# Running a heavy and a light expert of a mixture-of-experts kernel together, block by block in turns

## The chip, the cores and the metric

The kernel runs on one core of a Trainium2 chip. The metric is device time in microseconds (us) from start to end of one execution; lower is better. Engines are named as in the profile: PE is TensorE's matmul stream, DVE is VectorE, ACT is ScalarE, POOL is GpSimd and SP is SyncE, which here issues the loads of the weights.

## The reference

Two layers of an encoder over 256 tokens of width 1024. Each layer is a token mixer and then a channel mixer; the second layer's channel mixer sends each token to 2 of 8 experts. The change touches only those experts:

```python
def swiglu(h, w1, w3, w2):
    return (jax.nn.silu(h @ w1) * (h @ w3)) @ w2
...
    for e in range(N_EXPERTS):
        out = out + combine[..., e:e + 1] * swiglu(h, w1[e], w3[e], w2[e])
```

An expert has w1 and w3 of 1024 x 3584 and w2 of 3584 x 1024, all in float32.

## The kernel before

The experts are ordered by load and run as eight phases with the roles `ROLES = "HLHLHLHH"`: a heavy phase (H: 0, 2, 4, 6, 7) has 128 slots for tokens, a light one (L: 1, 3, 5) has 64. The hidden width of 3584 is cut into `NM` = 7 blocks of 512. A block needs w1 (two halves), w3 (two halves) and w2 (two halves): six **items** of 128 x 2048 floats, 1 MiB each, so 336 items in all.

Each item goes through four steps. SP loads it into one of 7 buffers `raw`. ACT copies it, rounded, to `whi`, line L1726. DVE computes the remainder `wlo` = raw - whi, line L2381. PE then multiplies with both. `whi` and `wlo` have only `SPLIT` = 3 buffers each, so ACT may write `whi` of item n only when PE has finished item n - 3, and SP may reload a `raw` buffer when the `wlo` of item n - 7 is done.

The number of matmuls of an item depends on the role. In a heavy phase the tokens' rows are split into a high and a low part, and an item takes 12 matmuls of 128 x 512 (hi x whi, lo x whi, hi x wlo). In a light phase both parts of the 64 rows lie side by side in the 128 columns, and an item takes 8 (L1187, L1191 for w1 and w3, L1230 for w2).

PE goes through the blocks in the order: w1 of block b (bank 0, group "e1"), transpose of the hidden values of block b - 1 (bank 2, "eT"), w3 of block b (bank 1, "e3"), w2 of block b - 1 (`down`, banks 4 and 5). Between them the other two engines work:

- heavy: ACT applies silu to bank 0 (L1737), DVE multiplies with bank 1 (`hidden`, L2394, the row `sgv<-sgv,bank`), PE transposes (L1210), ACT makes the high part (L1752), DVE the low part (`hidden_lo`, L2417, the row `yT_lo<-bank,yT_hi`). `down` waits for that low part before its first matmul, and for `wlo` of its own item.
- light: ACT copies bank 0 and bank 1 to SBUF (L1737, L1747), PE transposes and folds the 64-row halves together with 16 small matmuls (L1206), ACT applies silu (L1742), and DVE makes both parts with three instructions (L2407, L2410, L2412), which `down` waits for.

Which item each engine handles before which of these steps is set by `e_room`: an engine takes all items whose `whi` can become free before PE reaches the step in question. All engines work strictly through the order written in the program. In particular `hidden_lo` first does the `wlo` of every item up to three after the last one that PE finishes ahead of the transpose.

Between two experts, the new tokens' rows come back from memory (a DMA on ACT's queue), are transposed by PE (`rows_T`, L1250) and split by ACT and DVE; the old expert's result is copied out of banks 4 and 5 by ACT (L1845), for a light one folded by PE (`fold_result`, L1242) and copied again, and stored by a DMA on ACT's queue.

Of the kernel before, what the change touches and what calls it, by code (L numbers as in the profile page):

```python
# [42 lines left out]
CAP = 128  # L43
# [9 lines left out]
TWO_PI = 6.283185307179586  # L53

# [8 lines left out]
def plan_psum(depth, heads, x_heads, fcd, nblk, over_jobs):  # L63
# [16 lines left out]
    for l in range(depth):  # L80
# [69 lines left out]
        else:  # L150
# [14 lines left out]
            for p in range(last + 1):  # L165
                for b in range(1, nblk):
                    give(p, "e1", b, 0)
                    if b == 1 and p and ROLES[p - 1] == "L":
                        for n in range(2):
                            give(p - 1, "yf", n, 6 + n)  # L170
                    give(p, "eT", b - 1, 2)
                    if b == nblk - 1 and p < last:
                        for n in range(2):
                            give(p + 1, "rows", n, 7 - n)
                    give(p, "e3", b, 1)
                    if b == 1:
                        for n in range(2):
                            give(p, "ey", n, 4 + n)
                if p < last:
                    give(p + 1, "e1", 0, 0)  # L180
                    give(p, "eT", nblk - 1, 2)
                    give(p + 1, "e3", 0, 1)
                else:
                    give(p, "eT", nblk - 1, 2)
                    give(p, "selT", 0, 3)
                    for n in range(4):
                        give(p, "scatter", n, n)
# [59 lines left out]
def build(nc, x, mem, positions, g_mix, w_in, g_q, g_kv, w_uq, w_uk, w_uv, g_sg, w_s, b_s, g_mem,  # L247
# [31 lines left out]
    with ExitStack() as ctx:  # L279
# [105 lines left out]
        hselT = [v[:, :, 2:4, :].rearrange("p n a s -> p n (a s)") for v in yT]  # L385

# [92 lines left out]
        slots_moved = sem("slots_moved")  # L479
# [94 lines left out]

        e_items = head_items(0)
        for p in range(NE):
            e_items += mid_items(p) + (head_items(p + 1) if p < LAST else []) + halves(p, ("w2", NM - 1))
# [99 lines left out]
        def e_room(phase, kind, n):  # L677

            limit = marks[phase, kind, n][0]
            start, end = (N_E, N_E + PER_E) if phase == "over" else (0, N_E)  # L680
            i = start + SPLIT
            while i < end and marks["item", i - SPLIT][0] < limit:
                i += 1
            return i

# [12 lines left out]
        def _(pe):  # L698
# [470 lines left out]
            def up(phase, kind, b_, j=0, rows=None):  # L1169
# [3 lines left out]
                for half in range(2):  # L1173
# [10 lines left out]
                    for k, a in order:  # L1184
                        if rows is not None and phase == 0 and k == 0:
                            rows(half) if a else pe.wait_ge(rows_hi, half + 1)
                        nc.tensor.matmul(b[:, :], hselT[a][:, half, tok(k)], w[:, k, :],  # L1187
                                         start=(half + k + a == 0), stop=False)
                    w = e_part(wlo, lo_ready, n, j)
                    for k in range(4):  # L1190
                        ins = nc.tensor.matmul(b[:, :], hselT[0][:, half, tok(k)], w[:, k, :],  # L1191
# [21 lines left out]
            def down(phase, b_, j=0, halves=(0, 1)):  # L1213
# [6 lines left out]
                for half in halves:  # L1220
# [24 lines left out]
            def rows_T(phase, j=0):  # L1245

                for n in range(2):
                    b = claim((phase, "rows", n), j)
                    for c in range(4):
                        ins = nc.tensor.transpose(b[:, c * CAP:(c + 1) * CAP], row_in_slot[:, tok(4 * n + c)], ident[:, :])  # L1250
                    mark(ins, (phase, "rows", n))

            def blocks(phase, j=0):

                for b_ in range(1, NM):
                    up(phase, "w1", b_, j)
                    if b_ == 1 and phase != "over" and phase and light[phase - 1]:
                        fold_result(phase - 1)
                    hidden_T(phase, b_ - 1, j)
                    if phase != "over" and phase < LAST and b_ == NM - 1:  # L1260

                        pe.wait_ge(slots_moved, 32 * phase + 16)
                        rows_T(phase + 1)
# [47 lines left out]
            with pe.If(overflow > 0):  # L1311
                before, names = count, set(marks)
                with pe.Fori(0, OVER) as j:
                    pe.wait_ge(slots_moved, 16 * j + 16 * (2 * NE - 1))
                    rows_T("over", j)
# [83 lines left out]
        def _(pool):  # L1399
# [69 lines left out]
            pool.wait_ge(slots_moved, 32 * (NE - 1))  # L1469
# [7 lines left out]
        def _(act):  # L1477
# [276 lines left out]
            def rows_hi_part(phase, j=0):  # L1754

                for n in range(2):
                    b = full(act, (phase, "rows", n), j)
                    if is_light(phase):
                        ins = nc.scalar.activation(by_slot(hselT[0][:, n, :])[:, :, 0:LIGHT],
                                                   by_slot(b[:, :])[:, :, 0:LIGHT], ACT.Copy)  # L1760
                    else:
                        ins = nc.scalar.activation(hselT[0][:, n, :], b[:, :], ACT.Copy)
                    ins.then_inc(rows_hi, 1)

            def store_result(p):

                if light[p]:
# [3 lines left out]
                    for n in range(2):  # L1771
                        read(act, (p, "yf", n))
                else:
                    for n in range(2):
                        read(act, (p, "ey", n))
                act.dma_start(y_by_slot[p], y_slot).then_inc(slots_moved, 16)

            def blocks(phase, j=0):

                for b_ in range(1, NM):  # L1780
                    e_hi(e_room(phase, "e1", b_), j)
                    if is_light(phase):
                        e_hi(e_room(phase, "eT", b_ - 1), j)
                        silu_folded(phase, b_ - 1)
                    e_silu(phase, b_, j)
                    if b_ == 1 and phase != "over" and phase and light[phase - 1]:
                        store_result(phase - 1)
                    if phase != "over" and phase < LAST and b_ == (4 if phase else 5):

                        act.wait_ge(dispatched, 16 * 2 * T)  # L1790
                        if phase:
                            reached(act, (phase, "rows", 1))
                        act.dma_start(row_in_slot, rows_by_slot[phase + 1]).then_inc(slots_moved, 16)
                    e_hi(e_room(phase, "eT", b_ - 1), j)
                    if is_light(phase):
                        e_hi(e_room(phase, "e3", b_))
                        copy_gate(phase, b_)
                    else:
                        hidden_hi(phase, b_ - 1, j)
# [23 lines left out]
            for p in range(NE - 1):  # L1823
                blocks(p)

                e_hi(e_room(p, "e3", NM - 1))
                reached(act, (p, "e3", NM - 1))
                rows_hi_part(p + 1)
                e_hi(e_room(p + 1, "e1", 0))
                if light[p]:  # L1830
                    e_hi(e_room(p, "eT", NM - 1))
                    silu_folded(p, NM - 1)
                e_silu(p + 1, 0)
                if not light[p]:
                    e_hi(e_room(p, "eT", NM - 1))
                    hidden_hi(p, NM - 1)
                if light[p + 1]:
                    e_hi(e_room(p + 1, "e3", 0))
# [751 lines left out]
```

## Time and profile before

| | us |
|---|---|
| median of 3 runs | 1623.9 (1622.59 to 1624.29) |
| the profiled execution | 1622.44 |
| its span | 1620.6 |
| PE / DVE / ACT busy | 1576.3 / 1278.0 / 1057.4 |
| experts 1 to 6, from w1 of expert 1 to the first half of w3 of expert 7 | 678.55 |

The profiled execution's own time is 1.84 us above its span and 1.5 us below the median. Matmul busy times overlap in the profile: what counts for PE is the distance from the start of one instruction to the start of the next. The last line of the table is the part of the program that the change reorders.

### The profile page before, as it was taken

The numbers are of one execution on the slowest core, as the hardware profiler recorded it, in microseconds if no ns is written. First come the engines' busy times: TensorE is split into PE (matmuls) and PEld (weight loads), VectorE is DVE, ScalarE is ACT, GpSimd is POOL, SyncE is SP. The second block draws the span as 40 slices with busy tenths as digits, with TensorE's granted clock in tenths as the row PEclk, the third lists the DMA queues.
The fourth block names the chain that finished last, engine by engine and source line by source line (L and its number), as shares of the span: only waits on it lengthen the run. The fifth ranks groups of instructions, "written<-read, shape, count | busy, mean of one in ns | idle before, by whom it ended". The sixth has DMA issues, their size and how long they took to land.

```text
span 1620.6 us, 21022 instructions
## 1 busy us (share of the span) xinstructions
PE 1576.3 (97%) x8224; PEld 1335.5 (82%) x8224; DVE 1278.0 (79%) x1204; ACT 1057.4 (65%) x988; POOL 28.6 (2%) x69
## 2 busy tenths in 40 slices
PE   9999999999999999999999999989999999999997
PEld 8988888999989888787877788777788777788885
DVE  7575666555576756689899988899888999888997
ACT  6555445333355554567788877788777888777774
POOL 1000000000000000001000000000000000000100
PEclk9999999999999999999999999999999999999998
DMA  7754478977455535669999999999999999999992
GB/s 239 223 185 142 143 250 279 303 245 233 127 165 174 181 117 182 250 259 364 423 421 420 421 419 391 368 422 420 422 398 374 401 420 421 412 394 352 409 397 114
DMA packets 143112, 497.48 MB, mean 307 GB/s; under 512 B 8534, under 2 KB 64400, under 8 KB 100000
## 3 DMA queue, kind: packets, MB, share of 16 engines
q1 hardware_dynamic: 137008, 479.23, 78.1%
q0 software_dynamic: 2624, 8.45, 1.5%
q10 hardware_dynamic: 3376, 8.39, 1.4%
q8 instruction: 68, 1.11, 0.3%
q14 instruction: 36, 0.29, 0.0%
HBM read 476.64 MB, written 19.40 MB: 306 GB/s over the span
## 4 chain that ended last, share of the span: by engine, by line
PE 71%; DVE 20%; ACT 4%; issue 4%; DMA 1%; ACTq 0%; POOL 0%; DVEq 0%; POOLq 0%
PE bank L730 21%; DVE wlo L2381 14%; PE bank L1187 14%; PE bank L1230 13%; PE bank L901 9%; PE bank L1191 7%; ACT whi L1726 2%; ACT whi L1493 1%; PE bank L720 1%; DVE wlo L1915 1%; PE bank L1015 1%; PE bank L1210 1%; PE bank L1206 1%; DMA hn<-in_mem 1%; ACT pbuf L1628 0%
## 5 line engine op out<-in xcount | busy, mean ns | idle before, releaser
L2381 DVE TENSOR_TENSOR wlo<-raw,whi 128x2048 fp32r<-128x2048 f32 x328 | 738.9, 2286 | 67.4 <-ACT whi L1726 67.1
L1726 ACT ACTIVATE whi<-raw 128x2048 fp32r<-128x2048 f32 x328 | 624.0, 1917 | 161.5 <-PE bank L1191 83.8
L1915 DVE TENSOR_TENSOR wlo<-raw,whi 128x2048 fp32r<-128x2048 f32 (+3 forms) x121 | 259.3, 2148 | 178.6 <-ACT whi L1493 177.2
L1187 PE MATMUL bank<-whi,yT_hi 128*128 128x512 f32 x896 | 311.9, 396 | 0.0
L1493 ACT ACTIVATE whi<-raw 128x2048 fp32r<-128x2048 f32 (+3 forms) x121 | 217.8, 1801 | 137.7 <-PE bank L730 101.3
L1191 PE MATMUL bank<-wlo,yT_hi 128*128 128x512 f32 x896 | 240.5, 390 | 0.1
L1187 PE MATMUL bank<-whi,yT_lo 128*128 128x512 f32 x560 | 216.5, 390 | 0.0
L1230 PE MATMUL bank<-whi,yT_hi 128*128 128x512 f32 x448 | 180.4, 403 | 26.1 <-DVE yT_hi L2412 16.0
L1191 PEld LDWEIGHTS bank<-wlo,yT_hi 128*128 128x128 f32 x896 | 167.8, 188 | 36.9 <-DVE wlo L2381 1.4
L1187 PEld LDWEIGHTS bank<-whi,yT_hi 128*128 128x128 f32 x896 | 166.7, 188 | 33.1
L1230 PE MATMUL bank<-wlo,yT_hi 128*128 128x512 f32 x448 | 175.9, 393 | 0.0
L1230 PEld LDWEIGHTS bank<-whi,yT_hi 128*128 128x128 f32 x448 | 84.6, 189 | 61.7 <-DVE yT_hi L2412 23.8
L730 PE MATMUL bank<-hT_hi,whi 128*128 128x256 f32 x464 | 131.4, 283 | 0.0
L730 PE MATMUL bank<-hT_hi,wlo 128*128 128x256 f32 x464 | 131.3, 283 | 0.0
L730 PE MATMUL bank<-hT_lo,whi 128*128 128x256 f32 x464 | 131.3, 283 | 0.0
L1187 PEld LDWEIGHTS bank<-whi,yT_lo 128*128 128x128 f32 x560 | 105.2, 188 | 21.2 <-DVE yT_lo L2298 0.2
L1230 PE MATMUL bank<-whi,yT_lo 128*128 128x512 f32 x280 | 109.1, 390 | 0.0
L1230 PEld LDWEIGHTS bank<-wlo,yT_hi 128*128 128x128 f32 x448 | 84.7, 189 | 16.9
L730 PEld LDWEIGHTS bank<-hT_lo,whi 128*128 128x128 f32 x464 | 89.0, 192 | 0.4
L730 PEld LDWEIGHTS bank<-hT_hi,whi 128*128 128x128 f32 x464 | 89.0, 192 | 0.4
L730 PEld LDWEIGHTS bank<-hT_hi,wlo 128*128 128x128 f32 x464 | 89.0, 192 | 0.0
L730 PE MATMUL bank<-whi,mT_hi 128*128 128x512 f32 (+1 forms) x204 | 79.6, 390 | 0.0
(323 smaller groups left out, 2059.2 us busy)
## 6 DMA issues: line engine op xcount, KB each, us to landing
raw<-in_moe_w SPq DMA_DIRECT2D x336, 1024.0 KB, 8.5
raw<-in_w_in SPq DMA_DIRECT2D x36, 1024.0 KB, 5.2
raw<-in_dense_w SPq DMA_DIRECT2D x30, 1024.0 KB, 6.6
raw<-in_w_br SPq DMA_DIRECT2D x12, 1024.0 KB, 5.0
rows_by_slot<-qxT SPq DMA_DIRECT2D x23, 512.0 KB, 7.2
raw<-in_w_out SPq DMA_DIRECT2D x8, 1024.0 KB, 5.0
raw<-in_w_mkv SPq DMA_DIRECT2D x6, 1024.0 KB, 8.4
cqkv<-rows_by_slot ACTq DMA_DIRECT2D x7, 512.0 KB, 7.9
```

The lines of the kernel that those rows point to most:

```text
L720: ins = nc.tensor.matmul(bank, lhs(k), rhs(k), start=(k == 0), stop=(k == n - 1))
L730: ins = nc.tensor.matmul(bank, lhs(a, k), rhs(b, k), start=(start and k == chunks[0] and a + b == 0), stop=(stop and k == chunks[-1] and a ...
L901: ins = nc.tensor.matmul(bank, src(a, x0), w[b_][:, w0, :], start=(start and q + i == 0), stop=(stop and last))
L1015: ins = nc.tensor.matmul(b[:, t * SEQ:(t + 1) * SEQ], qT[0:QK, h, tok(t)], kT[0:QK, h, :], start=True, stop=True)
L1187: nc.tensor.matmul(b[:, :], hselT[a][:, half, tok(k)], w[:, k, :], start=(half + k + a == 0), stop=False)
L1191: ins = nc.tensor.matmul(b[:, :], hselT[0][:, half, tok(k)], w[:, k, :], start=False, stop=(half == 1 and k == 3))
L1206: ins = nc.tensor.matmul(b[:, a:a + LIGHT], src[:, tok(c)], fold[:, 0:LIGHT], start=True, stop=True)
L1230: ins = nc.tensor.matmul(banks[4 + n][:, :], gated_m[a][:, b_ % 2, tok(2 * half + c)], w[p][:, c, n * HALF:(n + 1) * HALF], start=(b_ + ha ...
L1493: nc.scalar.activation(whi[:, m % SPLIT, 0:floats(n)], raw[:, pieces[n][1], 0:floats(n)], ACT.Copy).then_inc(hi_ready, 1)
L1726: nc.scalar.activation(whi[:, (E0 + n) % SPLIT, :], raw[:, n % RAW, :], ACT.Copy).then_inc(hi_ready, 1)
L1915: V.tensor_tensor(wlo[:, m % SPLIT, 0:size], raw[:, pieces[n][1], 0:size], whi[:, m % SPLIT, 0:size].bitcast(F32), ALU.subtract).then_inc( ...
L2381: V.tensor_tensor(wlo[:, s, :], raw[:, n % RAW, :], whi[:, s, :].bitcast(F32), ALU.subtract).then_inc(lo_ready, 1)
```

## The change

Phase 0 runs alone as before. Then phases 2 and 1 run together: block 0 of 2, block 0 of 1, block 1 of 2, block 1 of 1 and so on; then 4 and 3, then 6 and 5; phase 7 stands alone. Within a step PE's pattern stays: w1 of the new block, transpose of the block before it in the new order, w3 of the new block, w2 of the block before. Since both phases of a pair are live, the light one has its own buffers for its rows (`lselT`, `light_row`) and accumulates its result in banks 6 and 7 instead of 4 and 5, and the rows' transposes use bank 3. The semaphore for rows and results is split into three. The number of items, matmuls and bytes stays as it was. In phase 7 the four `add_picked` of DVE stand one block later.

```diff
+def block_order(nblk):
+    order = [(0, b) for b in range(nblk)]
+    for p in range(1, len(ROLES) - 1, 2):
+        order += [(q, b) for b in range(nblk) for q in (p + 1, p)]
+    return order + [(len(ROLES) - 1, b) for b in range(nblk)]
+
+def row_steps(nblk):
+    order = block_order(nblk)
+    mid, late = {}, {}
+    for p in range(1, len(ROLES)):
+        s = order.index((p, 0))
+        if s == nblk:
+            mid.setdefault(s - 1, []).extend([(p, 0), (p, 1)])
+        else:
+            late.setdefault(s - 2, []).append((p, 0))
+            mid.setdefault(s - 1, []).append((p, 1))
+    return mid, late
...
+        lselT = mT[0][:, 0:4, :].rearrange("p (n a) s -> p n (a s)", n=2)
+        light_row = qxT[:, :, :].rearrange("p k s -> p (k s)")
...
-        for p in range(NE):
-            e_items += mid_items(p) + (head_items(p + 1) if p < LAST else []) + halves(p, ("w2", NM - 1))
+        for (p, b), (q, c) in zip(order, order[1:]):
+            e_items += halves(q, ("w1", c), ("w3", c)) + halves(p, ("w2", b))
+        e_items += halves(LAST, ("w2", NM - 1))
...
-                                ins = nc.tensor.matmul(banks[4 + n][:, :], gated_m[a][:, b_ % 2, tok(2 * half + c)],
+                                ins = nc.tensor.matmul(banks[(6 if is_light(phase) else 4) + n][:, :], gated_m[a][:, b_ % 2, tok(2 * half + c)],
...
-            for p in range(NE):
-                blocks(p)
-                if p < LAST:
-                    up(p + 1, "w1", 0, 0, lambda half: read(pe, (p + 1, "rows", half)))
-                    hidden_T(p, NM - 1)
-                    up(p + 1, "w3", 0)
-                    down(p, NM - 1)
+            for i in range(1, SINGLE + 1):
+                (p, b_), (q, c) = order[i - 1:i + 1]
+                up(q, "w1", c, 0, None if c else lambda half: read(pe, (q, "rows", half)))
+                if folded(i) is not None:
+                    fold_result(folded(i))
+                hidden_T(p, b_)
+                for r, n in mid_rows.get(i, []):
+                    rows_T(r, n)
+                up(q, "w3", c)
+                for r, n in late_rows.get(i, []):
+                    rows_T(r, n)
+                down(p, b_)
+            blocks(LAST)
...
+            for i in range(1, SINGLE + 1):
+                (p, b_), (q, c) = order[i - 1:i + 1]
+                e_lo(e_room(q, "e1", c))
...
+                hidden_lo(p, b_)
...
+                e_lo(e_room(q, "e3", c))
...
+                hidden(q, c)
```

What this does to DVE's order, first **before, inside a heavy expert** (`sgv` is the product `hidden`, `yT_lo` the low part that `down` waits for; one block is a product, five `wlo`, a low part, one `wlo`):

```order
L2381 TENSOR_TENSOR wlo<-raw,whi 128x2048 x5
L2417 TENSOR_TENSOR yT_lo<-bank2,yT_hi 128x512
L2381 TENSOR_TENSOR wlo<-raw,whi 128x2048
L2394 TENSOR_TENSOR sgv<-sgv,bank1 128x512
L2381 TENSOR_TENSOR wlo<-raw,whi 128x2048 x5
```

Here the six `wlo` of a block are all of heavy items. DVE **before, inside a light expert** (one block is the three instructions of the light hidden values and six `wlo`):

```order
L2407 TENSOR_TENSOR cT<-cT,bank2 128x256
L2410 CAST yT_hi<-cT 128x4x64
L2412 TENSOR_TENSOR yT_hi<-cT,yT_hi 128x4x64
L2381 TENSOR_TENSOR wlo<-raw,whi 128x2048 x6
L2407 TENSOR_TENSOR cT<-cT,bank2 128x256
```

**After, inside a pair** (one turn of a heavy and a light block):

```order
L2458 TENSOR_TENSOR sgv<-sgv,bank1 128x512
L2445 TENSOR_TENSOR wlo<-raw,whi 128x2048 x5
L2481 TENSOR_TENSOR yT_lo<-bank2,yT_hi 128x512
L2445 TENSOR_TENSOR wlo<-raw,whi 128x2048 x6
L2471 TENSOR_TENSOR cT<-cT,bank2 128x256
L2474 CAST yT_hi<-cT 128x4x64
L2476 TENSOR_TENSOR yT_hi<-cT,yT_hi 128x4x64
L2445 TENSOR_TENSOR wlo<-raw,whi 128x2048
L2458 TENSOR_TENSOR sgv<-sgv,bank1 128x512
```

The first `wlo` run behind `sgv` here is of items w1 and w3 of the light block and the first half of w2 of the heavy one; then comes the heavy block's low part. So between the product and the low part of a heavy block five `wlo` stand as before, but four of them now belong to a light block, whose matmuls are fewer. The single `wlo` ahead of `sgv` is the second half of w2 of the light block, as it was of the heavy block before. The six in between are the second half of w2 of the heavy block, w1 and w3 of the next heavy block, and the first half of w2 of the light block.

ACT's order **before, inside a light expert** (`cT` is the folded silu, `sgv<-bank0` and `sgv<-bank1` the copies of e1 and e3):

```order
L1742 ACTIVATE cT<-bank2 128x256
L1737 ACTIVATE sgv<-bank0 128x512
L1726 ACTIVATE whi<-raw 128x2048
L1747 ACTIVATE sgv<-bank1 128x512
L1726 ACTIVATE whi<-raw 128x2048 x5
```

and **after, inside a pair** (`sgv<-bank0` is the heavy block's silu, then the light block's copy; `yT_hi` the heavy block's high part):

```order
L1793 ACTIVATE cT<-bank2 128x256
L1788 ACTIVATE sgv<-bank0 128x512
L1777 ACTIVATE whi<-raw 128x2048 x5
L1788 ACTIVATE sgv<-bank0 128x512
L1777 ACTIVATE whi<-raw 128x2048
L1803 ACTIVATE yT_hi<-bank2 128x512
L1777 ACTIVATE whi<-raw 128x2048
L1798 ACTIVATE sgv<-bank1 128x512
L1777 ACTIVATE whi<-raw 128x2048 x5
```

The run of five `whi` is one turn's second half of w2 of the light block and the next light block's w1 and w3; the single ones are the two halves of w2 of the heavy block. The small instructions of both roles now stand in one queue in turns.

## Rows read from the trace of the kernel before

**Rows 1.** The page: span; busy time, its share of the span and instructions of PE

```profile
span 1620.6 us, 21022 instructions
...
PE 1576.3 (97%) x8224; PEld 1335.5 (82%) x8224; DVE 1278.0 (79%) x1204; ACT 1057.4 (65%) x988; POOL 28.6 (2%) x69
```

**Rows 2.** Busy time by stretch: experts 1 to 6, inside heavy 2, inside light 3

```profile
core 0: us, PE busy (x) PEld busy (x) DVE busy (x) ACT busy (x) POOL busy (x), PEclk, DMA share, GB/s
811.46:1489.90 678.44, 653.00 (x3041) 530.76 (x3040) 622.99 (x373) 542.77 (x392) 0.00 (x0) 1.00 1.00 405
944.00:1028.00 84.00, 84.00 (x384) 69.64 (x385) 73.66 (x40) 61.86 (x40) 0.00 (x0) 1.00 1.00 400
1060.00:1118.00 58.00, 53.16 (x257) 42.56 (x257) 57.69 (x39) 49.36 (x37) 0.00 (x0) 1.00 1.01 422
```

**Rows 3.** Chain that ended last (start, length, work): two heavy, then two light blocks

```profile
994.63 5.44 PE bank L1230 x24
...
1011.44 5.44 PE bank L1230 x24
...
1060.63 10.40 DVE wlo L2381 x5
...
1074.96 10.36 DVE wlo L2381 x5
```

**Rows 4.** Timeline (start, length, work, wait): heavy expert, next item starts, whi, wlo

```profile
1189.23 0.39 PE L1187 MATMUL bank<-whi,yT_hi 128*128 128x512 f32 x1
...
1189.49 1.92 ACT L1726 ACTIVATE whi<-raw 128x2048 fp32r<-128x2048 f32 x1 [0.80 <-PE bank L1230]
...
1191.44 2.29 DVE L2381 TENSOR_TENSOR wlo<-raw,whi 128x2048 fp32r<-128x2048 f32 x1 [0.42 <-ACT whi L1726]
```

**Rows 5.** Timeline, step from light expert 1 to heavy expert 2

```profile
919.37 1.89 PE L1206 MATMUL bank<-cT,sgv 128*128 128x64 f32 x16
...
921.07 0.48 PE L1187 MATMUL bank<-whi,yT_hi 128*128 128x512 f32 x1
...
926.13 2.29 DVE L2381 TENSOR_TENSOR wlo<-raw,whi 128x2048 fp32r<-128x2048 f32 x1 [0.95 <-ACT whi L1726]
...
928.34 0.68 DVE L2394 TENSOR_TENSOR sgv<-sgv,bank 128x512 f32<-128x512 f32 x1
...
928.94 4.49 DVE L2381 TENSOR_TENSOR wlo<-raw,whi 128x2048 fp32r<-128x2048 f32 x2
```

**Rows 6.** Timeline, step from heavy expert 2 to light expert 3

```profile
1022.60 1.04 PE L1250 MATMUL bank<-ident,cqkv 128*128 128x128 f32 x8
...
1023.39 0.48 PE L1187 MATMUL bank<-whi,yT_hi 128*128 128x512 f32 x1
...
1034.39 1.07 PE L1187 MATMUL bank<-whi,yT_hi 128*128 128x512 f32 x4
...
1034.65 3.73 ACT L1726 ACTIVATE whi<-raw 128x2048 fp32r<-128x2048 f32 x2 [0.80 <-PE bank L1230]
...
1036.60 6.70 DVE L2381 TENSOR_TENSOR wlo<-raw,whi 128x2048 fp32r<-128x2048 f32 x3 [0.21 <-ACT whi L1726]
...
1043.22 0.68 DVE L2417 TENSOR_TENSOR yT_lo<-bank,yT_hi 128x512 fp32r<-128x512 f32 x1
...
1043.96 0.50 PE L1230 MATMUL bank<-whi,yT_hi 128*128 128x512 f32 x1 [1.60 <-DVE yT_lo L2417]
```

**Rows 7.** Timeline, fold and store of light expert 1's result

```profile
935.94 1.88 PE L1242 MATMUL bank<-mv,cT 128*128 128x512 f32 x4
...
938.97 1.92 ACT L1726 ACTIVATE whi<-raw 128x2048 fp32r<-128x2048 f32 x1 [0.52 <-ACT mv L1770]
```

**Rows 8.** Groups by line, 790 to 1600 us: result copies

```profile
L1845 ACT ACTIVATE mv<-bank 128x512 f32<-128x512 f32 x14 | 7.9, 586 | 1.0 <-PE bank L1230 1.0
```

**Rows 9.** Timeline: w1 of expert 1; first half of expert 7's w3 ends

```profile
811.46 1.07 PE L1187 MATMUL bank<-whi,yT_hi 128*128 128x512 f32 x4
...
1490.01 0.39 PE L1187 MATMUL bank<-whi,yT_hi 128*128 128x512 f32 x1
```

More of the change, by code:

```diff
@@ L164, in plan_psum @@
             give(0, "e3", 0, 1)
[L165 to L187, printed above, removed]
+            order = block_order(nblk)
+            mid, late = row_steps(nblk)
+            for i in range(1, len(order)):
+                (p, b), (q, c) = order[i - 1:i + 1]
+                give(q, "e1", c, 0)
+                if i > 1 and order[i - 2][1] == nblk - 1 and ROLES[order[i - 2][0]] == "L":
+                    for n in range(2):
+                        give(order[i - 2][0], "yf", n, 6 + n)
+                give(p, "eT", b, 2)
+                for r, n in mid.get(i, []):
+                    give(r, "rows", n, 7 - n if i == nblk - 1 else 3)
+                give(q, "e3", c, 1)
+                for r, n in late.get(i, []):
+                    give(r, "rows", n, 3)
+                if b == 0:
+                    for n in range(2):
+                        give(p, "ey", n, (6 if ROLES[p] == "L" else 4) + n)
+            give(last, "eT", nblk - 1, 2)
+            give(last, "selT", 0, 3)
+            for n in range(4):
+                give(last, "scatter", n, n)
             start = list(used)
@@ L684, in e_room, with rows_at, fetched, folded @@
             return i
+        def rows_at(p):
+            return (lselT if light[p] else hselT[0]), sum(light[q] == light[p] for q in range(1, p + 1))
+        def fetched(p):
+            return order.index((p, 0)) - 4 if p > 2 else NM - 2
+        def folded(i):
+            p, b = order[i - 2] if i > 1 else (0, 0)
+            return p if b == NM - 1 and light[p] else None
+        nth_rows, n_rows = {}, T
+        for i in range(len(order)):
+            for name in mid_rows.get(i, []) + late_rows.get(i, []):
+                n_rows += 1
+                nth_rows[name] = n_rows
         def light_block(p, b):
@@ L1243, in fold_result, with rows_T @@
                          (p, "yf", n))
[L1245 to L1251, printed above, removed]
+            def rows_T(phase, n, j=0):
+                if phase != "over":
+                    pe.wait_ge(light_row_in if light[phase] else heavy_row_in, 16 * rows_at(phase)[1])
+                row = light_row if is_light(phase) else row_in_slot
+                b = claim((phase, "rows", n), j)
+                for c in range(4):
+                    ins = nc.tensor.transpose(b[:, c * CAP:(c + 1) * CAP], row[:, tok(4 * n + c)], ident[:, :])
+                mark(ins, (phase, "rows", n))
             def blocks(phase, j=0):
@@ L1752, in hidden_hi, with rows_hi_part @@
                 nc.scalar.activation(gated_m[0][:, b_ % 2, :], b[:, :], ACT.Copy).then_inc(g_hi, 1)
[L1754 to L1763, printed above, removed]
+            def rows_hi_part(phase, n, j=0):
+                b = full(act, (phase, "rows", n), j)
+                if is_light(phase):
+                    ins = nc.scalar.activation(by_slot(lselT[:, n, :])[:, :, 0:LIGHT], by_slot(b[:, :])[:, :, 0:LIGHT], ACT.Copy)
+                else:
+                    ins = nc.scalar.activation(hselT[0][:, n, :], b[:, :], ACT.Copy)
+                ins.then_inc(rows_hi, 1)
+            n_stored = 0
             def store_result(p):
+                nonlocal n_stored
+                kind = "yf" if light[p] else "ey"
                 if light[p]:
@@ L1781, in blocks @@
                     e_hi(e_room(phase, "e1", b_), j)
-                    if is_light(phase):
-                        e_hi(e_room(phase, "eT", b_ - 1), j)
-                        silu_folded(phase, b_ - 1)
                     e_silu(phase, b_, j)
[L1786 to L1793, printed above, removed]
-                    e_hi(e_room(phase, "eT", b_ - 1), j)
[L1795 to L1799, printed above, removed]
+                    if phase == LAST and b_ == 1:
+                        store_result(folded(SINGLE + 1))
+                    e_hi(e_room(phase, "eT", b_ - 1), j)
+                    hidden_hi(phase, b_ - 1, j)
                     if phase == LAST and b_ == 3:
@@ L2401, in hidden_lo @@
                 b = full(dve, (phase, "eT", b_), j)
-                count = NM * (NE if phase == "over" else phase) + b_ + 1 + NM * j
+                count = NM * NE + b_ + 1 + NM * j if phase == "over" else order.index((phase, b_)) + 1
                 if is_light(phase):
@@ L2533, in _ @@
                     select()
-                    rows_lo("over", j)
+                    for n in range(2):
+                        rows_lo("over", n, j)
                     n_done = N_E
```

186 lines of the change are left out of this document (109 added, 77 removed).

## The prediction

> **What bounds the kernel now.** I read the page first: PE is busy for 97% of the span [rows 1], which says little, because the busy times of pipelined matmuls overlap. The stretches come next. Inside heavy expert 2 PE is busy for all of 84 us and DVE for 74; inside light expert 3 DVE is busy for 57.69 of 58 us and PE for 53 [rows 2]. So the two kinds of expert have different limits, and the chain of waits says the same with the length of a block: heavy blocks hang on PE and repeat every 1011.44 - 994.63 = 16.81 us, light ones hang on DVE and repeat every 1074.96 - 1060.63 = 14.33 us [rows 3]. A heavy and a light block cost 31.14 us. The moves between experts come on top: experts 1 to 6 take 1490.01 - 811.46 = 678.55 us [rows 9], and 21 x 31.14 is 654 of them.
>
> The pieces of a block. A matmul of the experts takes 5.44 / 24 = 0.227 us from start to start [rows 3], so a heavy item (12) takes 2.72 us of PE and a light one (8) 1.81. The heavy transpose takes the rest, 16.81 - 6 x 2.72 = 0.49 us. The light transpose takes 921.07 - 919.37 = 1.70, and the matmul behind it starts up some 0.09 late, as the one at 1043.96 does (0.50 long instead of 0.39) [rows 5, 6]: 1.79. An item's way to PE: the next item starts at 1189.23, `whi` starts 0.26 later, takes 1.92, and `wlo` starts 0.03 behind it [rows 4]: 2.21 us from the end of item n - 3 to the start of `wlo` of n. Back to back, `wlo` follow each other every (6.70 - 2.29) / 2 = 2.205 us [rows 6], a small instruction starts 2.21 behind the start of a `wlo`, and `sgv` holds the next `wlo` up by 928.94 - 928.34 = 0.60 [rows 5].
>
> **What the change does to a turn.** It removes and adds no item, matmul or byte; all it does is order. I number a turn's items as PE takes them: 1 to 4 are w1 and w3 of the light block, 5 and 6 w2 of the heavy one, 7 to 10 w1 and w3 of the next heavy block, 11 and 12 w2 of the light one. The heavy transpose lies between 2 and 3, the light one between 8 and 9.
>
> Added up per engine a turn looks cheap. PE: 6 x 1.81 + 6 x 2.72 + 0.49 + 1.79 = 29.5 us. DVE: 12 x 2.205 = 26.5, two heavy steps of 0.60, and 14.33 - 6 x 2.205 = 1.10 for the light step, 28.8 us. DMA: 12.58 MB at the 422 GB/s that it moves in the light expert [rows 2] is 29.8 us. All are below 31.14.
>
> But three buffers hold the engines close together, and there is a loop of waits that a turn can't be shorter than. By the order after the change:
>
> 1. `whi` of 12 must wait until PE has finished 9; its `wlo` starts 2.21 us after that.
> 2. Behind it DVE has, in this order, the heavy product (2.21 after the start of `wlo` 12), `wlo` of 1 to 5 (0.60 for the product, four times 2.205, then 2.21), and the heavy low part (0.68 [rows 6]): 2.21 + 0.60 + 8.82 + 2.21 + 0.68 = 14.52 us without a gap.
> 3. PE's item 5 waits for that low part (0.06 to the start at 1043.96 [rows 6], 0.10 start-up). Then PE does 5, 6, 7, 8, the light transpose and 9: 0.16 + 5 x 2.72 + 1.79 = 15.55 us. And 9 releases the next turn's `whi` 12.
>
> The loop is 2.21 + 14.52 + 15.55 = **32.3 us a turn, against 31.14 now**: 1.14 us more. It mixes the slow leg of each kind: DVE at its full pace for seven instructions, then PE at the heavy pace while DVE waits for `whi`. Inside heavy blocks it can't arise, since there the six items past the product take PE 16.3 us and DVE is always early; inside light ones DVE never stops, so nothing but its own sum counts.
>
> Is step 2 really without a gap, and is nothing else later? With PE's end of 9 at 0: `whi` of 1 is ready at 4.9 (10 ends at 2.72), DVE wants it at 5.0. 11 ends at 4.5, 12 waits for its `wlo` and ends at about 6.4, so `whi` of 2, 3 and 4 are ready at 6.8, 8.7 and 10.7; DVE wants them at 7.2, 9.4 and 11.6. ACT then copies the light e1, which ends at 10.5 (about as long as a result copy, 0.59 [rows 8]), and has `whi` of 5 at 13.3; wanted at 13.8. PE ends item 4 at 14.9 and stands still until 16.8: 1.9 us in each turn. After that the `wlo` of 6, 7 and 8 are done 0.7 us or more before PE needs them. The light step's three instructions end about 2 us before PE wants 11. Loads: a turn of 32.3 us takes 390 GB/s, less than the 422 that the light expert draws, so no wait on DMA is added.
>
> This wait exists once already, at the step from a heavy to a light expert: `whi` at 1034.65, three `wlo` from 1036.60, low part at 1043.22, and PE stands for 1.60 us until 1043.96 [rows 6]. The order there is that of every turn from now on. It is the nearest row to the new case, and it is 1.60 rather than 1.9 because the two items before it were heavy ones.
>
> **The sum.** Up to the w1 at 811.46 little differs: four more row transposes for the second expert, half of 1023.39 - 1022.60 [rows 6], 0.4 us. From there to the end of 9 in expert 2: 2 x 2.72 + 0.49 + 2.72, and four row transposes: 9.1. Then 21 turns: 21 x 32.27 = 677.7. Surcharges at the ends of experts:
> - first turn: items 11 and 12 are heavy (the low part is then due 9.5 us after the end of 12 at 8.16, so 0.9 late), and two result copies of 0.59 [rows 8] delay `whi` of 3: 2.1.
> - each of the two changes of pair: row transposes, their high and low parts, and bank 3 that has to come free in between, on all three legs (I follow the order: +1.0 on DVE, because ACT's row copy holds up `whi` of 1; +1.15 at item 5; +0.4 behind 8): 2.6. In the next turn result copies and the fold, where `whi` comes 938.97 - 935.94 = 3.03 us after the fold's start [rows 7], so that of 5 is 1.6 late. 4.2 each, 8.4.
> - into expert 7: 1.0.
>
> Together 0.4 + 9.1 + 677.7 + 2.1 + 8.4 + 1.0 = 698.7 against 678.55: +20.2. Behind it the last `down` of the pair is a light one (-1.8), and the fold of expert 5 comes into expert 7 (1.72 from 935.94, and about 0.3): +0.2. With the profiled execution's own time, 1622.44 + 20.4 = 1642.8; from the median it is **1644 us**, 1.3% slower.
>
> Bounds. The surcharges have no row of their own: if they cost nothing the time is 11.5 us less, about 1632; if they cost twice what I say, 11.5 more, 1656. The loop itself is bounded from below by its own instructions, all of which have rows; what it may have on top is a few hand-overs of 0.03 to 0.3 us like those of an item's way to PE [rows 4].
>
> **A rule that says the opposite.** The rows show two regimes, one on PE and one on DVE [rows 2, 3]. The Trainium skill, page "Perfetto Trace Analysis", section "Optimization Strategy", says of kernels whose most-contended engine changes over time that performance may be improved by interleaving those regimes. That is this change, and it is the first rival. The sum by the rule would be that of the busiest resource; by the loop above it is not reached with three buffers.
>
> **Rivals.**
> 1. *The loads even out.* A turn costs its busiest sum, DMA's 29.8 us. For it: the three sums, all below 31.14. Then 21 x 29.8 = 625.8 + 21.0 is 646.8, 32 us less: 1592. It would need `whi` to run further ahead than item n - 3, and the row of 1.60 us [rows 6] speaks against it. The change pays as soon as a turn with its surcharges stays under 31.3 us. 4%.
> 2. *The single steps repeat as they are recorded.* The step to a light expert takes 15.1 us (1034.39 until item 6 ends at 1043.96 + 5.54), the one to a heavy expert, by its pieces, 4 x 2.72 + 1.79 + 2 x 1.81 + 0.1 = 16.4; a turn would be 31.5, if DVE came into each turn as early as it does there. That gives 21 x 0.8 less than my sum: 1628. Against it: items 11 and 12 are light in a turn, so PE reaches 5 sooner than DVE. 5%.
> 3. *More than the loop.* If the pauses of PE lowered its granted clock, or ACT, which alternates between both roles, came later than I follow, the turn would go to 33 us or more: 1660 and up. The granted clock is 1.00, the 2.4 GHz level, in the light expert too, where PE has 5 of 58 us free [rows 2]. 5%.
>
> **How the numbers follow.** The forecast has 86%; its range 1632 to 1657 comes from the surcharges, and I give 1631 to 1658, which leaves out about 2 in 10. A measurement tells 0.2% (3 us) from no change. Faster 0.05 (rival 1 and a little of rival 2), within 0.2% 0.04, slower 0.91.
>
> **What would show it.** In the chain of the changed kernel, landmarks in the middle of a pair should repeat every 32.3 us. PE should show a pause before the first matmul of the heavy `down` in each turn, put down to `yT_lo`, of 1.6 to 2 us, some 21 times, where it can occur only at the three steps from heavy to light now; `wlo` of 1 to 5 should stand back to back, and DVE should wait for `whi` in items 8 to 12. DVE should no longer be busy for all of any long stretch, and DMA's rate should lie at about 390 GB/s in the pairs. I am wrong if turns repeat under 31.2 us, if the pause stands elsewhere, or if the difference arises outside the pairs.

## The result, and the profile after

The changed kernel takes **1650.39 us** (median of 4 runs, 1648.31 to 1655.48), the kernel before 1623.36 (4 runs, 1622.59 to 1624.29): 1.0171 times as long, 95% interval 1.0158 to 1.0184. The forecast was 1644, with a range of 1631 to 1658. The profiled execution is the shortest of the four, 1648.31, and stands 25.9 us above that of before.

The page: span and busy times.

```profile
span 1646.5 us, 21021 instructions
...
PE 1588.0 (96%) x8224; PEld 1332.7 (81%) x8224; DVE 1279.9 (78%) x1204; ACT 1056.7 (64%) x988; POOL 29.1 (2%) x69
```

Against [rows 1] the page hardly moves: the same matmuls and the same work on DVE, and busy times within 12 us on PE and 2 on DVE, in a span that is 25.9 us longer. The stretches say more. Inside the pair of experts 2 and 1, and inside that of 4 and 3:

```profile
core 0: us, PE busy (x) PEld busy (x) DVE busy (x) ACT busy (x) POOL busy (x), PEclk, DMA share, GB/s
835.00:1000.00 165.00, 156.04 (x712) 123.76 (x712) 148.90 (x88) 127.65 (x89) 0.00 (x0) 1.00 0.98 393
1070.00:1235.00 165.00, 155.75 (x704) 123.64 (x705) 147.32 (x88) 126.34 (x88) 0.00 (x0) 0.99 0.98 390
```

Nothing is busy all the time any more: PE for 94 to 95%, DVE for 89 to 90%. DMA moves 390 to 393 GB/s. In [rows 2] PE was full in the heavy expert and DVE in the light one. The two regimes are mixed, and neither engine gained by it. The chain of waits (start, length, work), at the first matmuls of the heavy `down` in seven turns:

```profile
840.47 5.74 PE bank L1276 x24
872.81 5.74 PE bank L1276 x24
905.14 5.73 PE bank L1276 x24
937.47 5.74 PE bank L1276 x24
...
1070.84 7.34 PE bank L1276 x24
1104.77 5.74 PE bank L1276 x24
1137.11 5.73 PE bank L1276 x24
```

A turn takes 872.81 - 840.47 = 32.34 us, then 32.33, 32.33; where [rows 3] give 16.81 + 14.33 = 31.14 for the same two blocks. The row of 7.34 us is an exception, told below. One turn of the same chain, from item 9's last matmuls to item 5, shows which leg holds which:

```profile
1119.59 0.93 PE bank L1237 x4
1120.61 1.93 ACT whi L1777
1122.59 2.17 issue
1124.76 0.68 DVE sgv L2458
1125.44 8.64 DVE wlo L2445 x4
1134.09 0.08 issue
1134.17 2.29 DVE wlo L2445
1136.45 0.61 DVE yT_lo L2481
```

And the timeline of the same stretch, with what ended each wait:

```profile
1120.61 1.92 ACT L1777 ACTIVATE whi<-raw 128x2048 fp32r<-128x2048 f32 x1 [1.88 <-PE bank L1237]
...
1122.55 2.29 DVE L2445 TENSOR_TENSOR wlo<-raw,whi 128x2048 fp32r<-128x2048 f32 x1 [1.15 <-ACT whi L1777]
...
1124.76 0.68 DVE L2458 TENSOR_TENSOR sgv<-sgv,bank 128x512 f32<-128x512 f32 x1
...
1125.36 11.09 DVE L2445 TENSOR_TENSOR wlo<-raw,whi 128x2048 fp32r<-128x2048 f32 x5
...
1136.37 0.68 DVE L2481 TENSOR_TENSOR yT_lo<-bank,yT_hi 128x512 fp32r<-128x512 f32 x1
...
1137.11 0.50 PE L1276 MATMUL bank<-whi,yT_hi 128*128 128x512 f32 x1 [1.60 <-DVE yT_lo L2481]
```

ACT waits 1.88 us for PE's item 9 before the `whi` of 12, DVE 1.15 us for that `whi`; then DVE's `wlo` of 12, the product, the `wlo` of 1 to 5 and the low part follow without a gap, and PE has stood still for 1.60 us when the low part comes. PE's next five items and the light transpose, 1104.77 to 1120.52, release the next `whi`. The waits over 840 to 1500 us (engine, line, waited for: us in total, times, longest) put numbers on all turns together:

```profile
ACT whi L1777 <- PE bank L1237: 81.7, 75, 2.3
DVE wlo L2445 <- ACT whi L1777: 70.3, 100, 2.3
...
PE bank L1276 <- DVE yT_lo L2481: 31.0, 19, 2.0
```

PE's pause before the heavy `down` occurs 19 times and costs 31.0 us, 1.63 each. At the two changes of pair it lies ahead of the rows' transposes, which stand before `down` there (2.16 us each).

### The profile page after: what moved, and what is told of

It reads as the page before. It is cut to its first block, busy times and chain, and to the rows that moved or that the text cites. A ratio compares the mean times of both kernels' runs of the same rounds, so it can differ in the third digit from the quotient of the medians.

```text
span 1646.5 us, 21021 instructions
## 1 busy us (share of the span) xinstructions
PE 1588.0 (96%) x8224; PEld 1332.7 (81%) x8224; DVE 1279.9 (78%) x1204; ACT 1056.7 (64%) x988; POOL 29.1 (2%) x69
## 3 DMA queue, kind: packets, MB, share of 16 engines
q0 software_dynamic: 2624, 8.45, 1.5%
## 4 chain that ended last, share of the span: by engine, by line
PE 69%; DVE 20%; issue 5%; ACT 5%; ACTq 0%; DVEq 0%; POOL 0%; POOLq 0%
PE bank L776 22%; DVE wlo L2445 14%; PE bank L1233 12%; PE bank L1276 12%; PE bank L947 9%; PE bank L1237 6%; ACT whi L1777 3%; PE bank L1252 2%; ACT whi L1544 1%; DVE yT_lo L2481 1%; PE bank L766 1%; DVE wlo L1979 1%; PE bank L1061 1%; DVE sgv L2458 1%; ACT pbuf L1679 0%
## 5 line engine op out<-in xcount | busy, mean ns | idle before, releaser
L1233 PE MATMUL bank<-whi,yT_hi 128*128 128x512 f32 x560 | 219.8, 396 | 0.0
L1276 PE MATMUL bank<-whi,yT_hi 128*128 128x512 f32 x448 | 180.9, 404 | 32.3 <-DVE yT_lo L2481 31.9
L1276 PE MATMUL bank<-wlo,yT_hi 128*128 128x512 f32 x448 | 176.2, 393 | 0.0
L1237 PE MATMUL bank<-wlo,yT_hi 128*128 128x512 f32 x560 | 150.3, 390 | 0.0
L1276 PEld LDWEIGHTS bank<-whi,yT_hi 128*128 128x128 f32 x448 | 84.9, 189 | 65.6 <-DVE yT_lo L2481 42.4
L1237 PEld LDWEIGHTS bank<-wlo,yT_hi 128*128 128x128 f32 x560 | 105.0, 188 | 22.8 <-DVE wlo L2445 0.5
L1233 PEld LDWEIGHTS bank<-whi,yT_hi 128*128 128x128 f32 x560 | 105.2, 188 | 20.9
L1276 PEld LDWEIGHTS bank<-wlo,yT_hi 128*128 128x128 f32 x448 | 85.1, 190 | 17.6
L1237 PE MATMUL bank<-wlo,mT_hi 128*128 128x512 f32 x336 | 95.7, 406 | 2.9 <-DVE wlo L2445 1.2
L1233 PE MATMUL bank<-whi,mT_hi 128*128 128x512 f32 x336 | 92.4, 397 | 0.0
```

The source lines that it names most:

```text
L1233: nc.tensor.matmul(b[:, :], (lselT if is_light(phase) else hselT[a])[:, half, tok(k)], w[:, k, :], start=(half + k + a == 0), stop=False)
L1237: ins = nc.tensor.matmul(b[:, :], (lselT if is_light(phase) else hselT[0])[:, half, tok(k)], w[:, k, :], start=False, stop=(half == 1 and ...
L1276: ins = nc.tensor.matmul(banks[(6 if is_light(phase) else 4) + n][:, :], gated_m[a][:, b_ % 2, tok(2 * half + c)], w[p][:, c, n * HALF:(n ...
```

## The experiments

**1 to 3: a fourth `whi` buffer.** The loop of waits exists because `whi` of 12 may not be written before 9 is done. With four buffers it may be written once 8 is done. The fourth lies in a tile that is unused in this stage (`mT_lo`); `wlo` keeps three, so DVE now waits itself for item n - 3. The same edit in the kernel before is the control.

```diff
+        def hi_user(n):
+            return n - (4 if HEAD + EARLY + 3 <= n < N_E else SPLIT)
...
-                        reached(act, ("item", n - SPLIT), j)
-                    nc.scalar.activation(whi[:, (E0 + n) % SPLIT, :], raw[:, n % RAW, :], ACT.Copy).then_inc(hi_ready, 1)
+                        reached(act, ("item", hi_user(n)), j)
+                    nc.scalar.activation(whi_of(n), raw[:, n % RAW, :], ACT.Copy).then_inc(hi_ready, 1)
...
+                    if n < N_E:
+                        reached(dve, ("item", n - SPLIT))
```

The second of the three also moves ACT's copy of the light e1 behind the `whi` of item 5:

```diff
-                e_silu(q, c)
+                if not light[q]:
+                    e_silu(q, c)
...
+                if light[q]:
+                    e_silu(q, c)
```

Expected of the changed kernel with four `whi`:

> The changed kernel with a fourth buffer for whi (a tile that the experts don't use); wlo keeps three, so DVE now waits for PE's end of item n - 3 itself. The order of the instructions is as in the changed kernel. Loop of waits: whi of 12 is made while PE is still at 9, so wlo of 12 starts about 0.3 instead of 2.2 us behind the end of 9. Then ACT's copy of the light e1, which stands ahead of whi of 5 and waits for PE's item 2, is the next to hold: turn about 31.2 us instead of 32.3, time about 1626, with a shorter pause ahead of the heavy w2. Loads even out (rival): the buffers were never the limit and the turn stays at 32.3, about 1650. If the surplus was the granted clock alone: also about 1650.

Expected with the copy moved too:

> As the one before, and ACT's copy of the light e1 stands behind whi of item 5. Loop of waits: DVE's leg runs from 0.35 us behind the end of 9 without a gap, turn 30.4 us, about 40 us less than the changed kernel, 1609, which is faster than the kernel before. If the loads' sum of 29.8 us on DMA holds earlier, a turn of 30.5 or more and DVE waiting for ACT that waits for DMA. Rival (loads or clock): no change, 1650.

Expected of the control:

> Control: the kernel before with the same fourth buffer for whi. Heavy blocks hang on PE (16.81) and light ones on DVE (14.33), and neither waits for a buffer, so both stay. Only the three pauses at the steps from heavy to light go, 1.6 to 1.8 us each: about 1618. If a fourth buffer is worth as much here as in the pairs (rival: it helps everywhere), 1590 to 1600.

Measured, against 1623.13 of before: 1626.54 with four `whi` (1624.95 to 1629.98; ratio 1.0023, 1.0013 to 1.0032), 1620.97 with the copy moved (1619.40 to 1622.31; 0.9985, 0.9976 to 0.9995), and 1618.93 for the control (1617.82 to 1620.28; 0.9972, 0.9961 to 0.9983). So one more buffer takes 24 us off the changed kernel and 4 off the one before. That is the cause, taken away: the change's loss was the loop through `whi`. The timeline of DVE with four `whi`, low parts in two turns:

```profile
1096.01 0.68 DVE L2493 TENSOR_TENSOR yT_lo<-bank,yT_hi 128x512 fp32r<-128x512 f32 x1
...
1127.14 0.68 DVE L2493 TENSOR_TENSOR yT_lo<-bank,yT_hi 128x512 fp32r<-128x512 f32 x1
```

A turn takes 31.13 us, 1.20 less than 32.33, and 21 turns make 25.2 us. Its two changes of pair give 3.3 of them back: they cost 7.4 us each over two plain turns, where the changed kernel's cost 11.5 together. That leaves 21.9, where the two profiled executions lie 21.8 apart. What holds the turn now is in the rows between them, on ACT and DVE, ahead of the low part of 1127.14:

```profile
1122.49 0.60 ACT L1798 ACTIVATE sgv<-bank 128x512 f32<-128x512 f32 x1 [1.65 <-PE bank L1247]
1122.98 1.91 ACT L1787 ACTIVATE whi<-raw 128x2048 fp32r<-128x2048 f32 x1
...
1124.93 2.29 DVE L2457 TENSOR_TENSOR wlo<-raw,whi 128x2048 fp32r<-128x2048 f32 x1 [0.20 <-ACT whi L1787]
```

ACT waits 1.65 us for PE to finish item 2, to copy the light block's e1, and only then comes to the `whi` of 5. The second kernel takes that away, and its turn is 30.84 us, where 30.4 was expected. The miss is in DVE's rows:

```profile
1110.89 2.29 DVE L2460 TENSOR_TENSOR wlo<-raw,whi 128x2048 fp32r<-128x2048 f32 x1 [1.14 <-PE bank L1247]
1113.54 0.69 DVE L2473 TENSOR_TENSOR sgv<-sgv,bank 128x512 f32<-128x512 f32 x1 [0.36 <-PE bank L1247]
```

DVE now waits for PE in front of `wlo` and of the heavy product, which needs item 10's bank. The wait had moved to the three `wlo` buffers and the product. The turns' 0.44 us are 9.2 of the 12 us by which the total missed 1609. The two changes of pair are 2.8 more: they cost 7.9 and 6.4 us over two plain turns, 14.3 where the changed kernel's cost 11.5.

**4 and 5: less work on DVE, on the loop and off it.** Both leave out half of some of DVE's small instructions, and with that part of the computation, as their expectations say. The first halves the heavy product and low part, which lie on the loop; the second halves the light block's three instructions, which do not.

```diff
-                free(V.tensor_tensor(part[1], b[:, :], part[0].bitcast(F32), ALU.subtract), (phase, "eT", b_))
+                w = HALF if phase in ("over", 0, LAST) else HALF // 2
+                free(V.tensor_tensor(part[1][:, 0:w], b[:, 0:w], part[0][:, 0:w].bitcast(F32), ALU.subtract), (phase, "eT", b_))
```

```diff
-                    V.tensor_copy(part[:, :, 0:LIGHT], by_chunk).then_inc(g_hi, 1)
+                    V.tensor_copy(part[:, 0:2, 0:LIGHT], by_chunk[:, 0:2, :]).then_inc(g_hi, 1)
```

Expected of the half on the loop:

> The changed kernel; for experts 1 to 6 DVE makes only 256 of the 512 columns of the heavy product and of the heavy low part (this leaves out half of both). It takes 0.27 us from each of two DVE instructions that lie on the loop of waits: turn 32.33 - 0.54 = 31.8 us, 21 turns, 11 us less. If DVE's total load or nothing of DVE decided: 0.

Expected of the half off it:

> The changed kernel; DVE makes only half of each of its three instructions for the light block's hidden values (this leaves out half of them). About 0.4 us a turn less of DVE's load, but they stand ahead of wlo of 12, where DVE waits for whi anyway: turn unchanged at 32.33, time within 1 us but for pauses that lower the granted clock. If DVE's total load decided: 8 us less.

Single runs: 1643.11 and 1659.01. The turn of the first, by DVE's timeline:

```profile
1103.51 0.42 DVE L2483 TENSOR_TENSOR yT_lo<-bank,yT_hi 128x256 fp32r<-128x256 f32 x1
...
1135.49 0.42 DVE L2483 TENSOR_TENSOR yT_lo<-bank,yT_hi 128x256 fp32r<-128x256 f32 x1
```

is 31.98 us, 0.35 less, where 31.8 was expected. The low part's 0.26 us come through in full; of the product's share only 0.09, and there the `whi` of 1 is in the way: in the changed kernel ACT finishes it 0.1 us before the `wlo` of 1 starts. The second kernel's turns are 32.33 us, or 33.94 in seven of them: work off the loop gives nothing back. The total missed the expected 1650 by 9 us, and not by DVE's doing: DVE is busy for less, and the granted clock is 0.97 in the stretch below. Its trace has eight falls of the clock of 1.6 us, seven in those turns and one at a change of pair, six more than the changed kernel's, which is 9.7 us; experiments 8 to 10 go after it.

```profile
core 0: us, PE busy (x) PEld busy (x) DVE busy (x) ACT busy (x) POOL busy (x), PEclk, DMA share, GB/s
1070.00:1235.00 165.00, 156.11 (x693) 123.86 (x692) 140.87 (x85) 122.96 (x84) 0.00 (x0) 0.97 0.98 380
```

**6 and 7: the changed code in another order.** The changed kernel with no pair in turns (experts 0, 2, 1, 4, 3, 6, 5, 7 one after another), and with one pair in turns:

```diff
-        order += [(q, b) for b in range(nblk) for q in (p + 1, p)]
+        if p < 2:
+            order += [(q, b) for b in range(nblk) for q in (p + 1, p)]
+        else:
+            order += [(q, b) for q in (p + 1, p) for b in range(nblk)]
```

(with `p < 0` for none). Expected with none:

> The changed kernel's code with its extra buffers, banks and row transposes, but the experts one after the other: 0, 2, 1, 4, 3, 6, 5, 7. Blocks again 16.81 and 14.33 us. If the loss is the turns alone: 1621 to 1626, as the kernel before. If it is in what the pairs need beside the order (rows in bank 3, split semaphores, banks 6 and 7): still above 1635.

Expected with one:

> As the one before, but the pair 2 and 1 is run in turns, the rest one after the other. Seven turns: 7 x 1.19 = 8.3 us and about 2 us of surcharge above the sequential version: 1631 to 1636. If the loss came with the changes between pairs and not with turns, about 1625.

Single runs, before 1624.18 beside them: 1625.81 with none, 1634.26 with one pair. Without turns almost the whole loss is gone, so the new buffers, banks and semaphores cost at most 1.6 us; one pair costs 8.45 more, and its turns are 32.33 us in the trace. Three times 8.45 on top of 1625.81 is 1651.2, beside the measured 1650.39.

**8: four buffers of both.** The second kernel, with a fourth `wlo` buffer too (in `hT_lo`, until some 72 items before the end) and the heavy product behind the `wlo` of 1:

```diff
+                        reached(dve, ("item", n - (4 if HEAD + EARLY + 3 <= n < M4 else SPLIT)))
...
-                e_lo(e_room(q, "e3", c))
+                e_lo(e_room(q, "e3", c) + int(0 < q < LAST and not light[q]))
```

> The second version with four whi buffers (light copy behind whi of item 5), and with a fourth buffer for wlo as well, and the heavy product one wlo later on DVE. In that version the turn took 30.84 us because DVE's product, which needs PE's item 10, stood ahead of the next turn's wlo of 1 and everything behind it. Loop of waits: with the product behind wlo of 1, the leg from the end of 10 is shorter by one wlo less what it waited: turn 30.0 to 30.2, time about 1605. Sum of the DMA's load: 29.8 at the least. If the product was not the holder: 30.84 again, 1621.

**9: keep PE at work in the pause.** The changed kernel with eight products of a constant 128 x 128 tile into bank 3, which is free there, ahead of the heavy `down`, except at changes of pair:

```diff
+                if light[q] and not light[p] and not late_rows.get(i) and not mid_rows.get(i):
+                    read(pe, in3)
+                    for _ in range(8):
+                        nc.tensor.matmul(banks[3][:, 0:P], ident[:, :], ident[:, :], start=True, stop=True)
```

> The changed kernel, and in each light step of a pair but those at a change of pair PE does eight more matmuls of 128 x 128 on constants (into bank 3, read by nobody) ahead of the heavy w2, about 0.9 us inside its pause. Turn unchanged at 32.33, since the pause ends with DVE's low part. If the pauses are what lowers the granted clock, no group of w2 matmuls takes 7.3 us instead of 5.7, the runs lie closer together and the median falls by 3 to 5 us, to about 1646. If the clock falls for another reason: 1650 with the same spread; if the added matmuls don't fit into the pause: 1655 and more.

**10: the changed kernel again**, beside these two.

> The changed kernel as it is, beside the one with the added matmuls, for the spread of its runs: 1648 to 1656, each fall of the granted clock worth 1.6 us.

Measured, against 1623.64 of before: four of both 1616.15 (1615.44 to 1619.01; ratio 0.9952, 0.9935 to 0.9969); PE kept at work 1646.94 (1646.12 to 1648.20; 1.0146, 1.0129 to 1.0163); unchanged 1656.86 (1650.16 to 1658.27; 1.0190, 1.0168 to 1.0213).

With four of both a turn takes 30.26 us by two low parts on DVE, and 30.20 to 30.25 in most others, at the upper end of the 30.0 to 30.2 expected; the window shows DVE busy for 96% and DMA at 418 GB/s, near the 422 of [rows 2]:

```profile
1123.74 0.69 DVE L2507 TENSOR_TENSOR yT_lo<-bank,yT_hi 128x512 fp32r<-128x512 f32 x1
...
1154.00 0.69 DVE L2507 TENSOR_TENSOR yT_lo<-bank,yT_hi 128x512 fp32r<-128x512 f32 x1
```

```profile
core 0: us, PE busy (x) PEld busy (x) DVE busy (x) ACT busy (x) POOL busy (x), PEclk, DMA share, GB/s
1090.00:1220.00 130.00, 128.03 (x599) 105.43 (x598) 124.65 (x74) 106.31 (x75) 0.00 (x0) 1.00 1.01 418
```

So the turns reach what the sums per resource promised, within half a microsecond of the 29.8 us of DMA. The total missed 1605 by 11 us all the same. Part of the gain is given back at the changes of pair: there two turns together take 70.8 us, 10.4 over two plain ones, and 20.8 at both changes, against 14.3 in the second version. Rows of the first change, the last of them from the chain of waits:

```profile
1012.17 0.60 ACT L1832 ACTIVATE yT_hi<-bank 128x512 fp32r<-128x512 f32 x1 [3.31 <-PE bank L1319]
...
1014.60 2.29 DVE L2471 TENSOR_TENSOR wlo<-raw,whi 128x2048 fp32r<-128x2048 f32 x1 [3.41 <-ACT whi L1798]
...
1029.10 6.84 PE bank L1297 x24
```

ACT's high part of the new rows stands ahead of the next `whi` in its order and waits 3.31 us for PE's transposes of the rows (L1319), and DVE waits 3.41 us for the `whi` behind it. In the changed kernel the same instruction of ACT waits 1.19 us. The heavy `down` at this change takes 6.84 us, where it takes 5.47 at the changed kernel's change of pair: a fall of the clock, as told below. No run moved the high part of the rows, so what a better change of pair would give is open.

This version is 7.5 us under the kernel before, and 2.8 under the control, which was timed in another series and has a fourth buffer for `whi` alone. The kernel before with a fourth buffer for both was not run, so what the order in turns is worth beyond its buffers is not shown by the totals. For a gain of the order itself speaks the turn: 30.2 us against 31.14 for the same two blocks, in which PE (heavy) and DVE (light) were already busy all the time [rows 2].

The clock. In the changed kernel PE's pause is sometimes followed by matmuls at half speed. Timeline, four matmuls of the `down` at 1070.84:

```profile
1070.84 0.50 PE L1276 MATMUL bank<-whi,yT_hi 128*128 128x512 f32 x1 [1.96 <-DVE yT_lo L2481]
...
1073.15 0.63 PE L1276 MATMUL bank<-whi,yT_lo 128*128 128x512 f32 x1
1073.58 0.63 PE L1276 MATMUL bank<-wlo,yT_hi 128*128 128x512 f32 x1
...
1075.52 0.39 PE L1276 MATMUL bank<-whi,yT_lo 128*128 128x512 f32 x1
```

The windows around it, with the granted clock in the third column from the end:

```profile
1066.00:1071.00 5.00, 3.04 (x14) 2.22 (x13) 3.42 (x4) 5.00 (x5) 0.00 (x0) 1.00 0.95 366
1071.00:1075.00 4.00, 4.00 (x12) 3.17 (x13) 4.00 (x2) 1.43 (x1) 0.00 (x0) 0.61 1.02 427
```

Matmuls stand 0.43 us apart in place of 0.23 for eight of them, with a granted clock of 0.61 over the four microseconds, mostly the 1.2 GHz level: 7.34 - 5.74 = 1.60 us more for the 24. It occurs twice in this execution, both times one turn after a change of pair. In the repeat (profiled execution 1658.27, its span 10.0 us longer) it occurs eight times, and there behind an ordinary pause too:

```profile
874.46 0.53 PE L1276 MATMUL bank<-whi,yT_hi 128*128 128x512 f32 x1 [1.61 <-DVE yT_lo L2481]
...
875.22 0.63 PE L1276 MATMUL bank<-wlo,yT_hi 128*128 128x512 f32 x1
```

Six more times 1.61 us is 9.7 of the 10.0. The eight executions of the changed kernel, four in each series, go the same way: the mean granted clock is 0.994 to 0.995 in those of 1648 to 1650 us, 0.992 in the one of 1652, and 0.989 to 0.990 in those of 1655 to 1658. With PE kept at work, by its timeline and its window, the pause is filled and the clock stays at its upper level:

```profile
1133.36 1.95 PE L1362 MATMUL bank<-ident 128*128 128x128 f32 x16
1135.12 0.49 PE L1276 MATMUL bank<-whi,yT_hi 128*128 128x512 f32 x1
```

```profile
core 0: us, PE busy (x) PEld busy (x) DVE busy (x) ACT busy (x) POOL busy (x), PEclk, DMA share, GB/s
1070.00:1235.00 165.00, 164.35 (x795) 133.81 (x794) 148.93 (x88) 126.14 (x87) 0.00 (x0) 1.00 0.99 394
```

The eight products stand in the trace as 16 matmuls and last some 1.8 us, not the 0.9 expected: they fill the whole pause, and just fit. The turn is 32.34 us, as in the changed kernel. One fall is left in the stretch of the pairs, at a change of pair, where nothing was filled in. The median is 9.9 us under that of the repeat, and its runs lie within 2.1 us of each other, not 8.1. So the loop and the clock are two costs, each shown by itself: the filler takes the second away and leaves the first.

## Why the prediction was right, and where its sizes were off

The forecast's mechanism held, and the time lay in its range, 6 us above the predicted value.

- **The loop.** 32.33 us measured, 32.27 predicted. Its legs differ a little more: PE's 15.75 us (1104.77 to 1120.52) against 15.49 from the first matmul of item 5 to the end of 9, since each `down` after a pause takes 5.74 us and not 5.44 + 0.10; the way to the `wlo` of 12 is 2.03 (1122.55 - 1120.52) and not 2.21; DVE's 14.50 (1122.55 to 1137.05) against 14.52; 0.06 between them. The four give 32.34. One more `whi` buffer removes it, and halving the low part shortens it by the low part's own 0.26 us.
- **The sum, against the profiled execution.** From the w1 of expert 2 to the end of item 9 there: 9.1 predicted, 9.06 measured. The 21 turns: 21 x 32.33 = 678.9, where 677.7 was predicted. The first turn's surcharge: 2.0 for 2.1. Into expert 7: 0.8 for 1.0. The changes of pair: 5.6 and 5.9, where 4.2 each was predicted; 1.6 of each is the clock's fall, and without it they are 8.3 together for 8.4. Ahead of expert 2: 1.2 us for 0.4. The tail: 0.7 for 0.2. In all 25.9 for 20.4 (the terms as rounded here leave out 0.3 of it), and 3.2 of the 5.5 between them are the two falls of the clock.
- **The mis-sized term** is thus that of the clock, which the sum had at nothing and the third rival named ("if the pauses of PE lowered its granted clock"). The rival as it was put, turns of 33 us and more, did not come: most turns have the plain 32.33. But two to eight of them cost 1.6 us more, which is the spread from 1648 to 1658 and why the median stands further from the forecast than the shortest run. The range had been made for the surcharges and had no room for the clock. That the time lay in it was in part luck: the same kernel timed again had a median of 1656.86 and a longest run of 1658.27, just past its upper end.
- **The signs.** The pause was expected 21 times and 1.6 to 2 us long; it is listed 19 times, at 1.63 on average, and at the two changes of pair ahead of the rows' transposes. The estimate of 1.9 is too long by 0.3: the low part ends so that `down` starts 16.59 us behind the end of 9, not 16.8, because the way to the `wlo` of 12 is shorter, and PE ends item 4 at 15.0 and not 14.9. DMA at 390 GB/s was predicted, 390 and 393 measured.
- **The first rival** (loads even out, 1592) is refuted for this kernel and was right about the ceiling: with four buffers of both splits the turn falls to 30.26 us, where it had 29.8. The Trainium skill, page "Perfetto Trace Analysis", section "Optimization Strategy", says that interleaving regimes may improve performance; the runs here agree only with that version, which gains 0.5%, and with three buffers the same order loses 1.7%. The same section of the Trainium skill says that consistent bubbles can mean that there isn't room for the next tile; the pause of 1.6 us in every turn, together with 24 us from one buffer, is such a case.
- **The second rival** (turns of 31.5) is refuted: turns are 32.33 throughout.

Left open, besides the changes of pair of the last version: what of the 0.8 us ahead of expert 2 and the 0.5 us of the tail is order and what is spread between executions, and why the clock falls in some turns and not in others with the same pause.

## What to carry to other kernels

Sums per engine are a ceiling, not a forecast: where a few buffers tie the engines together, follow the order around once and add up the instructions from one release to the next. Mixing work bound by one engine with work bound by another needs buffers between them that let each run ahead by the difference; with three it made a loop of the slow leg of each, with four of both splits the turn was 0.9 us shorter than the two blocks one after another. When a buffer is added, expect the next wait right behind it, and time the old order with the same buffer beside it: here the old order with one more buffer has 4.2 us of the 7.5 that the new one gains with two.

## What the runs showed of the hardware that was not expected

A pause of PE of 1.6 to 2.2 us, in a stretch where it works for 94 to 95% of the time, was followed in 2 of 21 turns of one execution and in 8 of another by a fall of the granted clock to its 1.2 GHz level for some eight matmuls, 1.6 us each time; the same pause of 1.6 us was followed by none in other turns (the row of 1137.11, whose 24 matmuls take 5.73 us), and by none at two of the steps of the kernel before ([rows 6] has one; the granted clock is 1.00 over the 4 us from 1044). Filling the pause with eight small products left one fall in the pairs of an execution, and took 9.9 us off the median. Why the clock falls in one turn and not in the next is not known from these runs.
